# Two low parts of weight slabs made by GpSimd instead of VectorE in the latent attention

## The chip, the cores and the metric

The kernel runs on one core of a Trainium2 chip. The metric is the time of one execution in microseconds (us), the median of several runs. TensorE multiplies matrices, VectorE (DVE in the profile), ScalarE (ACT) and GpSimd (POOL) work on tiles in the on-chip memory SBUF, and SyncE (SP) issues transfers. VectorE and ScalarE also read PSUM, TensorE's eight result banks ps0 to ps7. The engines run side by side and wait for one another by semaphores only.

## The reference

It is a small transformer of two blocks over 256 tokens of width 1024, all in float32. The part that matters here is the first layer of the first block: eight heads of neighbourhood attention and eight heads of dense "latent" attention, joined and multiplied by an output weight. Beside it the second block's memory is normalized and projected.

```python
def dense_attention(q, k, v, scale):
    ...
        sc = jnp.einsum('bqhd,bkhd->bhqk', qi, k, preferred_element_type=jnp.float32) * scale
        p = jax.nn.softmax(sc, axis=-1)
        return jnp.einsum('bhqk,bkhd->bqhd', p.astype(v.dtype), v)
...
    return jnp.concatenate([out_a, out_b], axis=-1) @ w_o
...
        mkv = rms_norm_2(mem, mem_norm_gain[l]) @ w_mem_kv[l]
```

## The kernel before, in words

**Weights in slabs.** All weights pass through SBUF in 192 slabs of up to 128 x 2048 numbers, in the order of `weight_plan`. SyncE loads slab n into `raw[n % 5]`, once the products that used slab n - 5 are done. float32 products are made in two parts: ScalarE copies the slab to the reduced format as its high part (`whi`, L1230, three buffers), and the difference raw - whi is the low part (`wlo`, five buffers). VectorE makes it in one instruction of 128 x 2048 (L1720 in its `low`), or GpSimd in four of 128 x 512 (L2486 in its own `low`). `pooled(n)` says which of the two makes slab n's: in the kernel before GpSimd makes those of the last two slabs of `od_o`, most of `branch`, and all of `out2` and `fg`, all far behind the stage of the change. TensorE multiplies high by high, high by low and low by high (L595).

**When.** Each engine's program is written out by hand, and every step calls `ahead(n)`, which makes the parts of slab n + 2. A call for a slab that the engine doesn't make issues nothing. Slabs 10, 12, 15 and 17 (`EVO`) are the output weight of the first layer, and 11, 13, 14 and 16 (`MEM`) the memory's weight. So slab 14 is the third memory slab and slab 15 the third output slab.

**The attention around them.** Sixteen heads ("units" 0 to 15; from 8 on they are latent) pass in 19 steps s. Scores of a pair of units (L792 on TensorE); row maxima from PSUM (L1795 on VectorE for the latent ones); exponentials (L1296, ScalarE); one reciprocal and two multiplications of 128 x 256 per unit by 1/sum, from SBUF to SBUF (L1801, L1804 `TENSOR_SCALAR`, VectorE); transposes (L800, TensorE); a copy of the transposed probabilities from PSUM (VectorE's L1812 for odd units, ScalarE's L1305 for even ones); weighted values (L843, TensorE); outputs as a high part (L1326, ScalarE) and a low part (L1826, VectorE). Between these lie the products: step 11 multiplies slab 12 in four blocks, which VectorE adds to the residual (`onto`, L1868, reading PSUM), step 13 slab 13, step 15 slab 14, step 16 slab 15. The eight PSUM banks are handed out in turn, and TensorE takes one only when its last result has been read.

VectorE makes the low part of slab 14 in step 11, between the second and third block of slab 12, and that of slab 15 in step 13:

```python
                        if j == 2 and k < 3:
                            ahead(EVO[k])
                        onto(EVO[k], j, j)
```

Of the kernel before, what the change touches and what calls it, by code (L numbers as in the profile page):

```python
# [330 lines left out]
EVO = (10, 12, 15, 17)  # L331
MEM = (11, 13, 14, 16)
# [4 lines left out]
def build(nc, A, out):  # L337
    with ExitStack() as ctx:
# [124 lines left out]
        def pooled(n):  # L463

            name = plan[n][0]
            if name == "od_o":
                return n >= ODO + 2
            if name == "branch":
                return sum(p[0] == "branch" for p in plan[:n]) > 1
            return name in ("out2", "fg")  # L470
# [101 lines left out]
        def tensor(pe):  # L572
# [626 lines left out]
            for n in range(FF + 2, FD):  # L1199
                beside(n, x, late=pooled(n))  # L1200
                if n - FF in (4, 8, 12, 16):
                    rows_in((n - FF - 4) // 4)
# [509 lines left out]
        def vector(dve):  # L1712
            once = Once(dve)

            def low(n):
                if not split(n) or pooled(n):
                    return
                once.wait_ge(*at(("raw", n)))
                once.wait_ge(*at(("whi", n)))
                dve.tensor_tensor(wlo_of(n), raw_of(n), f32(whi_of(n)), ALU.subtract).then_inc(*tell(s_wlo, ("wlo", n)))  # L1720
# [754 lines left out]
        def gpsimd(pool):  # L2475
            once = Once(pool)

            def low(n):
                if not split(n) or not pooled(n):
                    return  # L2480
                once.wait_ge(*at(("raw", n)))
                once.wait_ge(*at(("whi", n)))
                lo, r, hi = wlo[n % RAW], raw[n % RAW], whi[split_at(n) % PARTS]
                for q in range(4):
                    v = slice(512 * q, 512 * q + 512)
                    m = pool.tensor_tensor(lo[:, v], r[:, v], f32(hi[:, v]), ALU.subtract)  # L2486
                m.then_inc(*tell(s_pool_wlo, ("wlo", n)))

            def ahead(n):
                for k in ahead_of(n):  # L2490
                    low(k)
# [49 lines left out]
                pool.tensor_tensor(QM[64:96, n, :], r[v, 0:256], r[v, 256:512], ALU.add).then_inc(*tell(s_pool, ("qr", n)))  # L2541
            once.wait_ge(*at(("qr", 7)))

            for n in (EVO[2], MEM[3], EVO[3]):
                ahead(n)
            for j in range(1, 4):
                add_square("n1", 0, j, j == 3)
# [44 lines left out]
            n = BLENDS  # L2592
# [90 lines left out]
        for program in (tensor, scalar, vector, gpsimd, sync):  # L2683
            program(silent)
# [8 lines left out]
        @block.gpsimd  # L2693
        def _(e):
            gpsimd(e)
# [39 lines left out]
```

## Time and profile before

| | |
|---|---|
| median of 3 runs | 1195.06 us (1194.7 to 1195.49) |
| the profiled execution | 1195.08 us |
| its span | 1193.3 us, TensorE clock granted 0.999 |
| TensorE busy | 1184.5 us |
| VectorE, ScalarE, GpSimd busy | 830.7, 658.5, 222.3 us |

The span runs from the first to the last instruction; 1.8 us of the execution lie around it. All times in rows are counted from the span's start. The latent attention with the memory's products beside it lies between about 80 and 150 us.

### The profile page before, as it was taken

How to read it: one execution, taken by the hardware profiler on the slowest of the kernel's cores; microseconds unless marked ns; L12 is line 12 of the kernel's file. 1: busy time of each engine (PE TensorE's matmuls, PEld its weight loads, DVE VectorE, ACT ScalarE, POOL GpSimd, SP SyncE). 2: the span in 40 equal slices, each digit the busy share in tenths (PEclk: the TensorE clock that was granted, in tenths of full speed). 3: DMA queues.
4: the chain of work that ended last, by engine and by line, in shares of the span. 5: the costliest groups of instructions: out<-in, count | busy, mean ns of one | idle time of the engine just before them, and what ended most of it. 6: DMA issues, size and time to landing. Idle time of an engine off the chain costs nothing.

```text
span 1193.3 us, 18415 instructions
## 1 busy us (share of the span) xinstructions
PE 1184.5 (99%) x7409; PEld 1034.6 (87%) x7409; DVE 830.7 (70%) x1184; ACT 658.5 (55%) x899; POOL 222.3 (19%) x169
## 2 busy tenths in 40 slices
PE   9999999999999999999999999999999999999998
PEld 9989898888898888888988888897878899888886
DVE  7878777754576688765788844597966566676863
ACT  5584465533455655557565535456685555555452
POOL 2530010000011021200300000010010885544100
PEclk9999999999999999999999999999999999999999
DMA  9723456656558566664366565555544455565551
GB/s 265 244 83 130 141 177 186 203 178 205 182 165 273 187 211 193 202 204 140 110 190 198 178 204 184 185 183 176 178 144 166 149 194 177 182 195 188 176 195 53
DMA packets 158995, 214.04 MB, mean 179 GB/s; under 512 B 5259, under 2 KB 111054, under 8 KB 158910
## 3 DMA queue, kind: packets, MB, share of 16 engines
q1 hardware_dynamic: 158110, 211.41, 54.6%
q8 instruction: 59, 0.97, 0.3%
q10 hardware_dynamic: 608, 0.99, 0.3%
q0 software_dynamic: 192, 0.46, 0.2%
q14 instruction: 26, 0.21, 0.1%
HBM read 205.50 MB, written 1.05 MB: 173 GB/s over the span
## 4 chain that ended last, share of the span: by engine, by line
PE 93%; DVE 4%; ACT 2%; issue 1%; DMA 1%; SPq 0%; DVEq 0%; ACTq 0%
PE ps L595 44%; PE ps L610 22%; PE ps L615 11%; PE ps L695 4%; PE ps L792 2%; PE ps L843 2%; PE ps L637 2%; PE ps L800 1%; DVE wlo L1720 1%; PE ps L811 1%; PE ps L661 1%; ACT whi L1230 1%; DMA raw<-in_ev_w_in_dram 1%; DVE TA L2400 0%; PE ps L716 0%
## 5 line engine op out<-in xcount | busy, mean ns | idle before, releaser
L1720 DVE TENSOR_TENSOR wlo<-raw,whi 128x2048 fp32r<-128x2048 f32 (+1 forms) x167 | 384.5, 2304 | 148.9 <-ACT whi L1230 148.3
L1230 ACT ACTIVATE whi<-raw 128x2048 fp32r<-128x2048 f32 x188 | 357.9, 1907 | 154.4 <-PE ps L595 132.3
L610 PE MATMUL ps<-XHL,whi 128*128 128x512 f32 x1248 | 311.1, 393 | 0.0
L610 PEld LDWEIGHTS ps<-XHL,whi 128*128 128x128 f32 x1248 | 225.3, 189 | 42.1 <-DVE BIG L2132 0.5
L615 PEld LDWEIGHTS ps<-XHL,wlo 128*128 128x128 f32 x1248 | 167.8, 190 | 11.8 <-DVE wlo L1720 1.1
L615 PE MATMUL ps<-XHL,wlo 128*128 128x256 f32 x1248 | 171.5, 282 | 0.3 <-DVE wlo L1720 0.2
L2486 POOL TENSOR_TENSOR wlo<-raw,whi 128x512 fp32r<-128x512 f32 x88 | 119.1, 1388 | 157.3 <-ACT whi L1230 157.1
L595 PE MATMUL ps<-whi,HL 128*128 128x512 f32 (+1 forms) x416 | 144.8, 373 | 0.0
L595 PE MATMUL ps<-whi,HH 128*128 128x512 f32 x384 | 143.3, 390 | 0.0
L595 PE MATMUL ps<-whi,XHL 128*128 128x512 f32 (+1 forms) x480 | 139.7, 378 | 0.0
L595 PE MATMUL ps<-wlo,HH 128*128 128x512 f32 x368 | 139.4, 389 | 0.0
L595 PEld LDWEIGHTS ps<-whi,XHL 128*128 128x128 f32 x480 | 85.9, 188 | 15.9 <-issue 0.7
L2562 POOL TENSOR_TENSOR TB<-TB,BIG 128x512 f32<-128x512 f32 x24 | 38.6, 1607 | 324.3 <-DVE BIG L2126 189.1
L595 PEld LDWEIGHTS ps<-whi,HL 128*128 128x128 f32 x416 | 76.1, 188 | 13.6
L595 PE MATMUL ps<-wlo,XHL 128*128 128x512 f32 (+1 forms) x240 | 87.8, 375 | 0.0
L595 PEld LDWEIGHTS ps<-whi,HH 128*128 128x128 f32 x384 | 71.9, 188 | 14.7
L595 PEld LDWEIGHTS ps<-wlo,HH 128*128 128x128 f32 x368 | 69.0, 188 | 14.6 <-DVE wlo L1720 0.4
L1286 ACT ACTIVATE TB<-ps 128x256 f32<-128x256 f32 x82 | 29.3, 378 | 58.0 <-PE ps L615 56.2
L1286 ACT ACTIVATE TA<-ps 128x256 f32<-128x256 f32 x66 | 23.4, 380 | 57.5 <-PE ps L615 45.1
L595 PEld LDWEIGHTS ps<-wlo,XHL 128*128 128x128 f32 x240 | 44.2, 188 | 8.3
L1861 DVE TENSOR_TENSOR TA<-ps,TB 128x256 f32<-128x256 f32 x56 | 23.2, 421 | 25.0 <-ACT TB L1286 24.7
L1296 ACT ACTIVATE SN<-SN,stat 128x384 f32<-128x384 f32 (+2 forms) x64 | 34.4, 544 | 10.1 <-DVE stat L1789 10.1
(281 smaller groups left out, 1652.6 us busy)
## 6 DMA issues: line engine op xcount, KB each, us to landing
raw<-in_mlp_w_dram SPq DMA_DIRECT2D x64, 1024.0 KB, 5.3
raw<-in_od_w_in_dram SPq DMA_DIRECT2D x36, 1024.0 KB, 5.4
raw<-in_w_in_dram SPq DMA_DIRECT2D x24, 1024.0 KB, 5.1
raw<-in_w_ffn_gate_dram SPq DMA_DIRECT2D x12, 1024.0 KB, 5.1
raw<-in_w_ffn_up_dram SPq DMA_DIRECT2D x12, 1024.0 KB, 5.1
raw<-in_w_ffn_down_dram SPq DMA_DIRECT2D x12, 1024.0 KB, 5.0
TB<-TA SPq DMA_DIRECT2D x96, 64.0 KB, 2.4
raw<-in_w_branch_dram SPq DMA_DIRECT2D x6, 1024.0 KB, 4.9
```

Source lines behind the costliest of these rows:

```text
L595: m = pe.matmul(to, l[c][a], r[c][b], start=first and k == 0, stop=last and k == 3 * n - 1)
L610: pe.matmul(b[m][:, :], w[m][c][0], XHL[:, c, :], start=c == 0, stop=False)
L615: i = pe.matmul(b[m][:, 0:S], w[m][c][1], x[c][0], start=False, stop=c == 7)
L637: i = pe.matmul(b[:, m * S:m * S + S], w[m][c][a], x[c][z], start=m == c == a == z == 0, stop=m == a == 1 and c == len(x) - 1)
L695: i = pe.matmul(b[n][:, m * S:m * S + S], h[a], x[c][z], start=m == c == a == z == 0, stop=m == 1 and c == 7 and z == 1)
L792: m = pe.matmul(banks[u][rows, lo:hi], l, r, start=start, stop=stop)
L1230: act.activation(whi_of(n), raw_of(n), ACT.Copy, scale=1.0).then_inc(*tell(s_whi, ("whi", n)))
L1286: act.activation(to[:, m * S:m * S + S], b[:, S:2 * S], ACT.Copy, scale=1.0).then_inc(*tell(s_act_out, ("copy", n, m)))
L1296: m = act.activation(to[:, lo:hi], src[:, lo:hi], ACT.Exp, bias=st[:, k:k + 1], scale=-1.0 if biased else 1.0, accum_out=st[:, 2 + k:3 + k])
L1720: dve.tensor_tensor(wlo_of(n), raw_of(n), f32(whi_of(n)), ALU.subtract).then_inc(*tell(s_wlo, ("wlo", n)))
L2486: m = pool.tensor_tensor(lo[:, v], r[:, v], f32(hi[:, v]), ALU.subtract)
L2562: pool.tensor_tensor(z, z, twice(RP[:, S:512]), ALU.mult).then_inc(*tell(s_pool, ("sine", k)))
```

## The change

`pooled` also names slabs 14 (`EVO[1] + 2`) and 15 (`MEM[1] + 2`). GpSimd's program calls `ahead(12)` and `ahead(13)` behind its last job in the latent attention, which issues these two low parts, four instructions each. The three calls that stood there, for slabs 17 to 19, issued nothing, as GpSimd made none of them. VectorE's calls stay and issue nothing for 14 and 15 now.

```diff
@@ -465,6 +465,8 @@
             name = plan[n][0]
             if name == "od_o":
                 return n >= ODO + 2
+            if n in (EVO[1] + 2, MEM[1] + 2):
+                return True
             if name == "branch":
                 return sum(p[0] == "branch" for p in plan[:n]) > 1
             return name in ("out2", "fg")
@@ -2541,7 +2543,7 @@
-            for n in (EVO[2], MEM[3], EVO[3]):
+            for n in (EVO[1], MEM[1]):
                 ahead(n)
             for j in range(1, 4):
                 add_square("n1", 0, j, j == 3)
```

All line numbers behind L466 grow by two. On VectorE, in step 11, this stands before: the scaling of unit 11, the four additions of slab 12's blocks with the low part of slab 14 (wlo4) between them, and the maxima of unit 12.

```order
L1804 TENSOR_SCALAR SN<-SN,stat 128x256 [waits s_dve]
L1804 TENSOR_SCALAR SN<-SN,stat 128x256
L1868 TENSOR_TENSOR XT<-XT,ps1 128x512 [waits s_product]
L1868 TENSOR_TENSOR XT<-XT,ps2 128x512 [waits s_product,s_dve_out]
L1720 TENSOR_TENSOR wlo4<-raw4,whi0 128x2048 [waits s_whi,s_raw4,s_dve_out]
L1868 TENSOR_TENSOR XT<-XT,ps3 128x512 [waits s_product]
L1868 TENSOR_TENSOR XT<-XT,ps4 128x512 [waits s_product,s_dve_out]
L1795 TENSOR_REDUCE stat<-ps5 128x1 [waits s_soft,s_score,s_dve_out]
```

And in the changed kernel, at the same place:

```order
L1806 TENSOR_SCALAR SN<-SN,stat 128x256 [waits s_dve]
L1806 TENSOR_SCALAR SN<-SN,stat 128x256
L1870 TENSOR_TENSOR XT<-XT,ps1 128x512 [waits s_product]
L1870 TENSOR_TENSOR XT<-XT,ps2 128x512 [waits s_product,s_dve_out]
L1870 TENSOR_TENSOR XT<-XT,ps3 128x512 [waits s_product,s_dve_out]
L1870 TENSOR_TENSOR XT<-XT,ps4 128x512 [waits s_product,s_dve_out]
L1797 TENSOR_REDUCE stat<-ps5 128x1 [waits s_soft,s_score,s_dve_out]
```

The low part is gone from VectorE and nothing else has moved; the same holds for slab 15 (wlo0) two steps on. On GpSimd the place between the queries' rotary sums (32x256) and the squares of the next norm (SQ) now has the two low parts:

```order
L2543 TENSOR_TENSOR BIG<-TB1 32x256 [waits s_pool] x3
L2488 TENSOR_TENSOR wlo4<-raw4,whi0 128x512 [waits s_whi,s_raw4,s_pool]
L2488 TENSOR_TENSOR wlo4<-raw4,whi0 128x512 x3
L2488 TENSOR_TENSOR wlo0<-raw0,whi1 128x512 [waits s_whi,s_raw0]
L2488 TENSOR_TENSOR wlo0<-raw0,whi1 128x512 x3
L2500 TENSOR_TENSOR SQ<-SQ 128x512 [waits s_square]
```

Before, the first and the last of these rows (L2541 and L2498 there) stood side by side. TensorE's order is the same in both kernels but for two semaphores. This is its stretch from the values of units 8 and 9 to the start of slab 13, in the kernel before:

```order
L843 MATMUL ps7<-PT,BIG 64x256 x3
L800 MATMUL ps0<-ident,SN 128x128 [waits s_soft]
L800 MATMUL ps0<-ident,SN 128x128 x3
L800 MATMUL ps1<-ident,SN 128x128 [waits s_soft,s_dve_out]
L800 MATMUL ps1<-ident,SN 128x128 x3
L595 MATMUL ps2<-HL,whi2 128x256 [waits s_whi,s_dve_out]
L595 MATMUL ps2<-HL,wlo3 128x256 [waits s_wlo]
```

The transposes of unit 11 (ps1) and slab 13's first product (ps2) wait for `s_dve_out`, which VectorE's additions above raise. Moved is only what TensorE waits for at the first low product of slabs 14 and 15: `s_pool_wlo` in place of `s_wlo`.

## Rows read from the trace of the kernel before

**Rows 1.** The page: busy time, share and instructions of each engine.

```profile
PE 1184.5 (99%) x7409; PEld 1034.6 (87%) x7409; DVE 830.7 (70%) x1184; ACT 658.5 (55%) x899; POOL 222.3 (19%) x169
```

**Rows 2.** Waits of TensorE, 84 to 160 us: total, times, longest.

```profile
PE ps L843 <- DVE PT L1812: 1.1, 2, 0.8
```

**Rows 3.** Timeline of TensorE: start, duration (us), instructions [idle before].

```profile
108.46 1.89 PE L792 MATMUL ps<-BIG 96*128 96x256 f32 x8
...
110.29 1.08 PE L843 MATMUL ps<-PT,BIG 128*64 128x256 f32 x8
111.30 1.09 PE L800 MATMUL ps<-ident,SN 128*128 128x128 f32 x8
112.15 0.36 PE L595 MATMUL ps<-HL,whi 128*128 128x256 f32 x1
...
117.99 1.89 PE L792 MATMUL ps<-BIG 96*128 96x256 f32 x8
120.18 1.08 PE L843 MATMUL ps<-PT,BIG 128*64 128x256 f32 x8 [0.30 <-DVE PT L1812]
121.20 1.09 PE L800 MATMUL ps<-ident,SN 128*128 128x128 f32 x8
...
128.88 1.08 PE L843 MATMUL ps<-PT,BIG 128*64 128x256 f32 x8 [0.85 <-DVE PT L1812]
```

**Rows 4.** Timeline of VectorE, 105 to 117 us.

```profile
105.55 2.29 DVE L1720 TENSOR_TENSOR wlo<-raw,whi 128x2048 fp32r<-128x2048 f32 x1
...
109.15 0.62 DVE L1804 TENSOR_SCALAR SN<-SN,stat 128x256 f32<-128x256 f32 x2
...
110.41 1.40 DVE L1868 TENSOR_TENSOR XT<-XT,ps 128x512 f32<-128x512 f32 x2
111.84 2.29 DVE L1720 TENSOR_TENSOR wlo<-raw,whi 128x2048 fp32r<-128x2048 f32 x1
114.06 1.40 DVE L1868 TENSOR_TENSOR XT<-XT,ps 128x512 f32<-128x512 f32 x2
115.49 1.42 DVE L1795 TENSOR_REDUCE stat<-ps 128x1 f32<-128x256 f32 x4
```

**Rows 5.** Timeline of VectorE, 120 to 129 us.

```profile
120.14 0.62 DVE L1804 TENSOR_SCALAR SN<-SN,stat 128x256 f32<-128x256 f32 x2
...
120.87 0.62 DVE L1804 TENSOR_SCALAR SN<-SN,stat 128x256 f32<-128x256 f32 x2
121.40 2.28 DVE L1720 TENSOR_TENSOR wlo<-raw,whi 128x2048 fp32r<-128x2048 f32 x1
...
124.20 1.41 DVE L1795 TENSOR_REDUCE stat<-ps 128x1 f32<-128x256 f32 x4
...
128.06 0.68 DVE L1812 COPY PT<-ps 128x512 f32<-128x512 f32 x1
```

**Rows 6.** Timeline of ScalarE: the high parts of slabs 13, 14 and of 15.

```profile
103.52 3.70 ACT L1230 ACTIVATE whi<-raw 128x2048 fp32r<-128x2048 f32 x2
...
118.84 1.94 ACT L1230 ACTIVATE whi<-raw 128x2048 fp32r<-128x2048 f32 x1
```

**Rows 7.** Timeline of GpSimd, 0 to 300 us: its next job.

```profile
152.45 1.30 POOL L2498 TENSOR_TENSOR SQ<-SQ 128x512 f32<-128x512 f32 x1 [72.29 <-ACT SQ L1246]
```

**Rows 8.** Timeline of GpSimd and VectorE side by side, 928 to 943 us.

```profile
928.42 10.07 POOL L2486 TENSOR_TENSOR wlo<-raw,whi 128x512 fp32r<-128x512 f32 x8 [49.33 <-ACT whi L1230]
...
928.23 1.64 DVE L1804 TENSOR_SCALAR SN<-SN,stat 128x256 f32<-128x256 f32 x2
930.84 0.42 DVE L1826 TENSOR_TENSOR OL<-ps,OH 128x256 fp32r<-128x256 f32 x1 [0.98 <-ACT OH L1326]
...
939.84 1.29 POOL L2486 TENSOR_TENSOR wlo<-raw,whi 128x512 fp32r<-128x512 f32 x1
...
940.24 1.44 DVE L2314 TENSOR_TENSOR BIG<-BIG,TB 128x512 f32<-128x512 f32 x1
...
941.10 1.75 POOL L2486 TENSOR_TENSOR wlo<-raw,whi 128x512 fp32r<-128x512 f32 x1
```

## The prediction

> **What bounds the kernel now.** I read the page's busy times first: TensorE is busy 1184.5 us of the 1193.3 us span, GpSimd 222.3 us [rows 1]. So nothing that shortens work on another engine pays unless TensorE waits for it. The change lies in the latent attention, so the next view is who TensorE waited for there, from 84 to 160 us: two waits, 1.1 us together, both of L843 (probabilities times values) for DVE's L1812, which copies transposed probabilities out of PSUM [rows 2]. The third view is TensorE in order of time [rows 3], where starts give each wait its size. Where it does not wait, the values follow the scores by 110.29 - 108.46 = 1.83 us; the next time by 120.18 - 117.99 = 2.19, so the first wait cost 0.36. A slab of this shape takes 117.99 - 112.15 = 5.84 us. The next slab starts 0.85 after the L800 of 121.20 (112.15 - 111.30), at 122.05, and ends at 127.89; the values start at 128.88, so the second wait cost 0.99. The sum, 1.35 us, is all that a faster DVE could win here; before and after these two TensorE goes on without a break.
>
> **What is removed.** Two DVE subtractions of 2.3 us, at 111.84 [rows 4] and at 121.40 [rows 5]. Both lie ahead of row maxima (L1795), on which the exponentials, the weighted values and then the late copy depend: 115.49 leads to the copy that L843 waits for at 120.18, and 124.20 to that of 128.06. Without anything else both copies would be some 2.2 us earlier and both waits gone.
>
> **What is added.** Eight GpSimd subtractions of a quarter slab. Their like appears later: eight in a row take 10.07 us, 1.26 each [rows 8], so a low part takes about 5.0 us in place of 2.29. They begin when ScalarE has written the high part: 103.52 + 3.70 = 107.22 for slab 14, and 118.84 + 1.94 = 120.78 for slab 15 [rows 6]. The low parts would be there by about 113 and 127; their slabs are multiplied from 122.05 and 130. So TensorE does not wait for GpSimd itself. The three removed calls of `ahead` issued no instruction, and GpSimd's next job starts at 152.45 after 72 us of idling [rows 7]: nothing is queued behind the new work. The change moves no DMA; weight loads are freed by the same products as before.
>
> **What it costs: DVE's scalings are held.** This is the term that I think decides. In [rows 8] a pair of L1804 (probabilities times 1/sum, SBUF to SBUF) takes 1.64 us beside a GpSimd subtraction, against 0.62 (109.15) without [rows 4]: the second of the pair ended at 928.23 + 1.64 = 929.87, 0.16 after the GpSimd instruction that was running (928.42, and 1.29 long as those at 939.84: 929.71). L2314, two SBUF inputs, ended at 941.68, 0.55 after the GpSimd instruction that began 0.4 us before it (939.84 + 1.29 = 941.13); the next GpSimd instruction ended at 942.85, 1.17 after L2314. L1826, which reads PSUM, took 0.42 in the middle of GpSimd's row. So DVE instructions with all operands in SBUF and GpSimd's subtractions take turns, one at a time, and those on PSUM pass. The Trainium skill says the same and more strictly (SBUF — State Buffer, "SBUF: two separate sides"): the pair of ports that the two engines share is an exclusive lock, held for the whole instruction, and the loser fully blocks. The trace agrees, with the 1.64 us above. Read at its worst, with each of four scalings held for a whole GpSimd instruction (4 x 1.26 = 5.0 us), the rule would give 2.2 us more than the sum below.
>
> First slab. DVE's previous subtraction ends at 105.55 + 2.29 = 107.84 [rows 4], after ScalarE's part, so GpSimd's first instruction really starts there and ends at 107.84 + 1.17 = 109.01. The first L1804 is issued at 109.15, when the second GpSimd instruction has begun (ends 110.27):
> - L1804 first: ends 110.27 + 0.15 = 110.42; GpSimd third: 110.42 + 1.17 = 111.59
> - L1804 second: 111.74; GpSimd fourth: 112.91
> - L1804 third: 113.06; the fourth finds GpSimd done and the next DVE instruction starts at 113.25.
> In the profile that next one (L1868, `onto`) starts at 110.41. So DVE is 2.84 us late there, and the 2.22 us saved behind it (114.06 - 111.84) leave it 0.62 late at the maxima: four L1868 of 0.715 bring 116.11 for 115.49.
>
> What waits for it: TensorE's order puts the transposes of unit 11 into bank ps1 and slab 13 into ps2, and takes each only after the first and the second L1868 have read it. The second ends at 113.25 + 0.71 + 0.68 = 114.64. Slab 13 started at 112.15 [rows 3], some 0.3 after its bank was freed by the L1868 that had ended by 111.84; TensorE follows a DVE result here after 0.14 (128.06 + 0.68 to 128.88). So slab 13 starts at 114.78: TensorE is 2.63 us late.
>
> What it gets back. The scores come at 117.99 + 2.63 = 120.62 and the values may start at 122.45; the copy L1812 had ended 0.14 before 120.18 and is only 0.62 late (120.66), so the first wait of 0.36 vanishes: 2.27 late. The second low part starts at about 120.9 + 0.62 on GpSimd, some 0.05 us after the third of four L1804 (120.87, [rows 5]), which shift by the same 0.62, as both hang on the same maxima. I take it that the fourth alone is held, by 1.02 as in [rows 8] (1.64 - 0.62). It then ends at 121.49 + 0.62 + 1.02 = 123.13, and the transposes that need it are due at 121.20 + 0.44 + 2.27 = 123.91: hidden by TensorE's own delay. The maxima come at 124.20 - 2.20 + 0.62 + 1.02 = 123.64 and the copy 3.86 (128.06 - 124.20) later, at 127.50, done by 128.2; slab 14 ends at 127.89 + 2.27 = 130.16. No wait: the second one (0.99) is gone too, and TensorE is 1.28 late. From there to the end it is busy without a break, with DVE and ScalarE ahead of it, so 1.28 us stays.
>
> Sum: +2.63 - 0.36 - 0.99 = +1.28. The profiled execution took 1195.08 us (span 1193.3 and 1.8 around it), the median of the runs is 1195.06, so I forecast **1196.3 us**. The bounds: nothing is held, -1.35; three or four scalings are held the second time too, +2.7 (below).
>
> **Rivals.**
> - *Banks free early enough.* If slab 13 waits only for the last scaling (113.33 + 0.14, then 0.43 of transposes: 113.90), TensorE is 1.75 late; 1.39 after the first wait is gone, and the transposes due at 121.20 + 0.44 + 1.39 = 123.03 wait 0.24 for 123.27. Less 0.99: +0.64, 1195.7 us. Against it: the order shows the wait of slab 13's first product for DVE's outputs.
> - *The engines don't disturb each other.* Both waits vanish, -1.35, 1193.7 us. For it: most DVE instructions here read PSUM, and 1.64 us in [rows 8] is one pair. Against it: the four scalings stand exactly where GpSimd starts.
> - *Held twice: slower.* The place is the second low part. If GpSimd's first instruction comes ahead of the softmax of unit 12 instead of just behind its third scaling, three are held, 2 x 1.02 more: the last ends at 125.17, and the transposes, due at 123.91, start at 125.31. TensorE is 2.27 + 1.40 = 3.67 late, and with the second wait gone 2.7: 1197.8 us. It decides if ScalarE is 0.8 us earlier against DVE (120.92 to 120.14); one scaling more, for which 0.06 us are enough, is +1.7 (1196.8). For it: 0.06 us is nothing. Against 0.8: the two move together.
> - *No effect at all*: held and hidden anyway, 1195.1 us. It would need slack at 112 us, where TensorE has none: the transposes started at 111.30, the scalings had ended 0.8 before.
>
> **How the numbers follow.** Forecast with its neighbours (1195.9 to 1196.9) 0.66; banks free early 0.10; undisturbed 0.10; held twice 0.08; no effect 0.06. The range of 8 in 10 takes in the first, the second and the last, and leaves out the undisturbed one and held twice: 1195.0 to 1197.3. What a measurement can tell here is about 0.2%, 2.39 us. The gain can't reach it, as TensorE's waits give 1.35 at most: faster 0.02 for what I overlook. Slower needs 2.39: held twice, 0.08. Same: 0.90.
>
> **What would show it.** L1804 near 109 as two pairs of about 2.4 and 1.5 us instead of 0.62; GpSimd's eight L2488 in two groups of about 5.1 us, near 108 and 121.5; TensorE's slab 13 starting about 2.6 us later, with a wait for DVE at L800 or the slab; no wait of L843 for L1812 at either place (L1814 now); everything from 130 us on shifted alike, by 1.3. I am wrong if L1804 keeps its 0.62, if TensorE waits for GpSimd's low parts at L597, or if the shift at 130 us differs from that at the end.

## The result

The changed kernel takes 1197.46 us (median of 20 runs, 1196.7 to 1199.46), the kernel before 1195.11 in the same series (20 runs, 1194.3 to 1196.56): a ratio of 1.002, 95% interval 1.0014 to 1.0027. It is 2.35 us slower where 1.28 was forecast, and just outside the range, which ended at 1197.3. The profiled execution took 1197.19 us (span 1195.4, 1.8 around it), 2.11 more than that of before.

**What became of TensorE and VectorE.** The page of the changed kernel, busy time of each engine:

```profile
PE 1185.3 (99%) x7409; PEld 1034.2 (87%) x7409; DVE 831.0 (70%) x1182; ACT 658.4 (55%) x899; POOL 232.8 (19%) x177
```

Against [rows 1] GpSimd has its eight instructions more, and VectorE two fewer. TensorE is 99% busy again, so the page alone tells nothing. The waits of TensorE from 84 to 160 us (total, times, longest), which answer to [rows 2]:

```profile
PE ps L802 <- DVE XT L1870: 1.5, 1, 1.5
PE ps L802 <- DVE SN L1806: 0.3, 1, 0.3
```

Both waits of L845 (L843 before) for the copy are gone, and two new ones stand at the transposes. TensorE in order of time (start, duration, instruction, idle before), against [rows 3]:

```profile
110.28 1.08 PE L845 MATMUL ps<-PT,BIG 128*64 128x256 f32 x8
111.68 0.66 PE L802 MATMUL ps<-ident,SN 128*128 128x128 f32 x4 [0.32 <-DVE SN L1806]
113.81 0.66 PE L802 MATMUL ps<-ident,SN 128*128 128x128 f32 x4 [1.47 <-DVE XT L1870]
114.53 0.39 PE L597 MATMUL ps<-HL,whi 128*128 128x256 f32 x1
...
120.38 1.89 PE L794 MATMUL ps<-BIG 96*128 96x256 f32 x8
122.20 1.08 PE L845 MATMUL ps<-PT,BIG 128*64 128x256 f32 x8
...
129.99 1.08 PE L845 MATMUL ps<-PT,BIG 128*64 128x256 f32 x8
```

Slab 13 starts at 114.53 for 112.15, 2.38 later. The values start at 122.20 for 120.18, 2.02 later: 0.36 came back. Those of 129.99 are 1.11 late. VectorE shows why (against [rows 4, 5]):

```profile
109.13 2.50 DVE L1806 TENSOR_SCALAR SN<-SN,stat 128x256 f32<-128x256 f32 x2
111.55 0.15 DVE L1803 RECIPROCAL stat<-stat 128x2 f32<-128x2 f32 x1
111.73 1.43 DVE L1806 TENSOR_SCALAR SN<-SN,stat 128x256 f32<-128x256 f32 x2
113.08 2.84 DVE L1870 TENSOR_TENSOR XT<-XT,ps 128x512 f32<-128x512 f32 x4
115.96 1.42 DVE L1797 TENSOR_REDUCE stat<-ps 128x1 f32<-128x256 f32 x4
...
120.60 0.62 DVE L1806 TENSOR_SCALAR SN<-SN,stat 128x256 f32<-128x256 f32 x2
121.13 0.16 DVE L1803 RECIPROCAL stat<-stat 128x2 f32<-128x2 f32 x1
121.33 1.63 DVE L1806 TENSOR_SCALAR SN<-SN,stat 128x256 f32<-128x256 f32 x2
```

and GpSimd's two new groups in the same execution:

```profile
107.38 5.37 POOL L2488 TENSOR_TENSOR wlo<-raw,whi 128x512 fp32r<-128x512 f32 x4 [27.21 <-ACT whi L1232]
121.38 5.21 POOL L2488 TENSOR_TENSOR wlo<-raw,whi 128x512 fp32r<-128x512 f32 x4 [8.64 <-ACT whi L1232]
```

The first four scalings take 2.50 and 1.43 us in place of 0.62 a pair, the second time one pair takes 1.63. One by one, the first three last 1.22, 1.35 and 1.17 us and end 0.15 us behind the end of a GpSimd instruction each (110.20, 111.48, 112.75); the fourth finds GpSimd done and takes 0.34. No semaphore stands between these instructions, so semaphores are not the only way in which engines hold each other up here. Up to 130 us the forecast's mechanism is what happened, with 1.11 us for 1.28. The text had said that everything behind would be shifted alike and that it was wrong if the shift at the end differed. It does: TensorE is 1.1 us late until 1099 us and 2.11 us late from 1106.

**Where the second microsecond goes.** Four views of the changed kernel near 1096 us: VectorE, GpSimd, ScalarE, TensorE.

```profile
1092.99 2.29 DVE L1722 TENSOR_TENSOR wlo<-raw,whi 128x2048 fp32r<-128x2048 f32 x1
1095.20 0.69 DVE L2419 TENSOR_TENSOR HL<-TB,HH 128x512 fp32r<-128x512 f32 x1
1096.27 0.76 DVE L1863 TENSOR_TENSOR TB<-ps,TB 128x256 f32<-128x256 f32 x2 [0.38 <-ACT TB L1288]
1097.06 1.77 DVE L2410 TENSOR_TENSOR TB<-TA,TB 128x512 f32<-128x512 f32 x1
...
1095.69 5.56 POOL L2488 TENSOR_TENSOR wlo<-raw,whi 128x512 fp32r<-128x512 f32 x4 [5.86 <-ACT whi L1232]
...
1095.46 0.64 ACT L1288 ACTIVATE TB<-ps 128x256 f32<-128x256 f32 x2
1098.87 0.63 ACT L1658 ACTIVATE HH<-TB 128x512 fp32r<-128x512 f32 x1 [2.78 <-DVE TB L2410]
...
1108.50 0.74 PE L617 MATMUL ps<-XHL,wlo 128*128 128x256 f32 x4 [0.80 <-DVE wlo L1722]
```

The same place in the kernel before:

```profile
1094.33 0.68 DVE L2417 TENSOR_TENSOR HL<-TB,HH 128x512 fp32r<-128x512 f32 x1
1095.05 0.76 DVE L1861 TENSOR_TENSOR TB<-ps,TB 128x256 f32<-128x256 f32 x2
1095.84 0.88 DVE L2408 TENSOR_TENSOR TB<-TA,TB 128x512 f32<-128x512 f32 x1
...
1094.83 5.55 POOL L2486 TENSOR_TENSOR wlo<-raw,whi 128x512 fp32r<-128x512 f32 x4 [5.88 <-ACT whi L1230]
...
1096.76 0.64 ACT L1656 ACTIVATE HH<-TB 128x512 fp32r<-128x512 f32 x1 [1.53 <-DVE TB L2408]
...
1106.39 1.21 PE L615 MATMUL ps<-XHL,wlo 128*128 128x256 f32 x8 [0.24 <-DVE wlo L1720]
```

In the changed kernel VectorE has a pause of 0.38 us ahead of L1863. The profile puts it down to ScalarE's L1288, but that had ended at 1096.10 and its first half earlier: the record of VectorE's wait for it ends at 1095.87, and L1863 starts 0.40 us behind that record, where the kernel before has 0.045 at the same place. Without the pause L2410 (both inputs in SBUF) meets the end of GpSimd's first quarter and takes 0.88; 0.38 later it meets the second quarter and is held as the scalings are: 1.77. ScalarE's HH, behind it, comes at 1098.87 for 1096.76, 1.25 us more than GpSimd's own shift there (0.86). ScalarE's and then VectorE's part of the next slab follow. TensorE, 1.13 us late against the kernel before until 1099 us, is 1.54 late at 1102, as its products there (L612) stretch by 0.41 behind the later ScalarE; then it waits 0.80 us for a low part instead of 0.24 and is 2.11 late. That is the whole 1.0.

What I then saw in counting: the instruction after the pause is the 1600th record of VectorE in the trace (its waits on semaphores are records too, so two low parts fewer are three records fewer, 1708 for 1711); the 1088th, 512 earlier, starts 0.4 us late too (hidden). Before, the 1600th is a low part three records earlier in the program, and starts on time, while the instruction ahead of it is still running. A third place shows the same in both kernels: the 448th record starts 0.41 us behind its wait's record before (300.46 us) and 0.40 in the changed kernel (303.39), though it is a different instruction of the program. The view of the DMA queues shows a packet on the queue for instruction code near either place (us 1098 to 1099 in the changed kernel; its columns are packets, MB, share of 16 engines):

```profile
q14 instruction: 1, 0.01, 2.1%
```

and from 1092 to 1093 us in the kernel before:

```profile
q14 instruction: 1, 0.01, 2.3%
```

The packet of the changed kernel lies between 1098.6 and 1099 us, more than 2 us behind the end of the pause (1096.27), and only14 below has one at 1094.3 without any pause near it. So the packets don't show that VectorE paused for code.

That made the theory for the late part: VectorE can pause at fixed numbers of its stream, and removing two instructions moves such a number onto a place where a pause costs. That it pauses for new code is a guess.

A third thing hides in the spread of the times. Of the 20 runs of the changed kernel seven have a mean granted clock of 0.998 or less and a median of 1198.46; the other thirteen have 1197.19. Of the kernel before, five of 66 runs in the two series below were so low, and not slower for it; a low mean is a sign of a clock drop, no proof. The profile of the changed kernel has no such drop; two of the kernels below were caught with one.

### The profile page after: what moved, and what is told of

It is laid out like the page before. It is cut to its first block, busy times and chain, and to the rows that moved or that the text cites. A ratio compares the mean times of both kernels' runs of the same rounds, so it can differ in the third digit from the quotient of the medians.

```text
span 1195.4 us, 18421 instructions
## 1 busy us (share of the span) xinstructions
PE 1185.3 (99%) x7409; PEld 1034.2 (87%) x7409; DVE 831.0 (70%) x1182; ACT 658.4 (55%) x899; POOL 232.8 (19%) x177
## 4 chain that ended last, share of the span: by engine, by line
PE 92%; DVE 3%; ACT 1%; DMA 1%; SPq 1%; issue 1%; DVEq 0%; ACTq 0%
PE ps L597 44%; PE ps L612 22%; PE ps L617 11%; PE ps L697 4%; PE ps L794 2%; PE ps L845 2%; PE ps L639 2%; PE ps L802 1%; DMA raw<-in_ev_w_in_dram 1%; ACT whi L1232 1%; PE ps L813 1%; DVE wlo L1722 1%; DVE TA L2402 0%; SPq L2640 0%; PE ps L1105 0%
## 5 line engine op out<-in xcount | busy, mean ns | idle before, releaser
L1722 DVE TENSOR_TENSOR wlo<-raw,whi 128x2048 fp32r<-128x2048 f32 (+1 forms) x165 | 379.9, 2304 | 148.2 <-ACT whi L1232 147.5
L612 PE MATMUL ps<-XHL,whi 128*128 128x512 f32 x1248 | 311.4, 393 | 0.2
L612 PEld LDWEIGHTS ps<-XHL,whi 128*128 128x128 f32 x1248 | 225.3, 189 | 42.5 <-ACT BIG L1672 0.5
L2488 POOL TENSOR_TENSOR wlo<-raw,whi 128x512 fp32r<-128x512 f32 x96 | 129.7, 1383 | 194.1 <-ACT whi L1232 193.9
L1288 ACT ACTIVATE TB<-ps 128x256 f32<-128x256 f32 x82 | 29.2, 377 | 58.0 <-PE ps L617 56.2
L1288 ACT ACTIVATE TA<-ps 128x256 f32<-128x256 f32 x66 | 23.4, 380 | 57.3 <-PE ps L617 45.0
L1863 DVE TENSOR_TENSOR TA<-ps,TB 128x256 f32<-128x256 f32 x56 | 23.2, 421 | 25.0 <-ACT TB L1288 24.7
```

The lines of the kernel that those rows point to most:

```text
L612: pe.matmul(b[m][:, :], w[m][c][0], XHL[:, c, :], start=c == 0, stop=False)
L1288: act.activation(to[:, m * S:m * S + S], b[:, S:2 * S], ACT.Copy, scale=1.0).then_inc(*tell(s_act_out, ("copy", n, m)))
```

## The experiments

Each kernel has 11 runs beside 33 of the kernel before on the same chip: 1195.00 us for the first four kernels, 1195.03 for the last four.

**only14: the first slab alone.** Against the changed kernel:

```diff
-            if n in (EVO[1] + 2, MEM[1] + 2):
+            if n == EVO[1] + 2:
```

> Only slab 14's low part goes to GpSimd; slab 15's stays on DVE. The collision theory: the four scalings near 109 us are held as in the changed kernel (pairs of about 2.5 and 1.4 us instead of 0.62), slab 13 starts 2.4 us late, both of TensorE's waits for the copies go, and TensorE is 1.0 to 1.1 us late at 130 us, like the changed kernel. If the engines did not disturb each other, it would be 0.36 us early there instead. Whether the end is as late as 130 us is the second question: if delays only add up, the time is 1196.2; if the later stages add the 1.2 us by which the changed kernel's median exceeds its shift at 130 us, it is 1197.4.

Measured: 1196.64 us (1195.76 to 1197.81), ratio 1.0012 (1.0003 to 1.0021). The waits near 112 us are the same 1.5 and 0.3 us. One instruction fewer instead of two puts the 1600th record on L2419, without a pause, and no wait of 0.8 us comes late (its 1088th record, a low part, does start 0.4 us late, hidden). But the profiled execution shows something else, in the table by stretch (busy time of each engine, then granted clock, DMA share, GB/s):

```profile
112.00:114.00 2.00, 0.65 (x4) 0.42 (x4) 1.97 (x4) 0.00 (x0) 0.28 (x1) 1.00 0.20 82
114.00:119.00 5.00, 4.94 (x29) 4.93 (x29) 2.80 (x7) 2.72 (x11) 0.00 (x0) 0.66 0.00 0
```

TensorE was busy 0.65 of 2.00 us, in its wait for L1870; then the granted clock averages 0.66 over five microseconds: half speed (the 1.2 GHz level) for 3.41 us from 114.61, with slab 13 under way. This execution loses 1.5 us more by it (TensorE, against the kernel before, from the start of slab 13 to the next scores). Five of the 11 runs have the low mean clock (median 1197.01), the others have 1196.06, which is +1.06, the theory's number. The split by clock was made after the runs were seen; the median of all 11 lies between the two forecasts.

**only15: the second slab alone.**

```diff
-            if n in (EVO[1] + 2, MEM[1] + 2):
+            if n == MEM[1] + 2:
```

> Only slab 15's low part goes to GpSimd; slab 14's stays on DVE. The collision theory: the scaling pair at 120.87 us takes 1.64 instead of 0.62, so the transposes of unit 13 start 1.0 us late, and the wait of 0.99 us for the copy near 128 us goes: no shift at 130 us, 1195.1 us. Without a disturbance the second wait alone would go: -0.99, 1194.1 us.

Measured: 1195.04 us (1194.02 to 1196.84), ratio 1.0 (0.9992 to 1.0009). TensorE's waits from 84 to 160 us:

```profile
PE ps L802 <- DVE SN L1806: 0.8, 1, 0.8
PE ps L845 <- DVE PT L1814: 0.3, 1, 0.3
```

One pair of scalings takes 1.62 us, the transposes wait 0.8 for it, and the late wait of L845 is paid for by that. So the second slab alone is worth nothing; in the changed kernel its cost is hidden by the lateness that the first one makes.

**after_scaling: GpSimd begins behind the scalings.** What disturbs is taken away, by order and not by size:

```diff
-            for n in (EVO[1], MEM[1]):
+            for n, u in ((EVO[1], 11), (MEM[1], 13)):
+                once.wait_ge(*at(("soft", u)))
                 ahead(n)
```

> Both low parts on GpSimd as in the changed kernel, but GpSimd starts each only when the scaling of units 10 and 11, and of 12 and 13, is done. The collision theory: L1806 keeps 0.62 us, the first low part runs from about 110.6 to 115.7, the second from 119.4 to 124.5, nothing of DVE's in these stretches has all its operands in SBUF, both waits of TensorE (1.35 us) go: 1193.7 us. If what costs is something else that a GpSimd subtraction does to DVE or to TensorE wherever it stands, it stays near the changed kernel's 1197.5.

Measured: 1194.99 us (1194.36 to 1196.91), ratio 0.9999 (0.999 to 1.0008). GpSimd's two groups in its timeline:

```profile
111.16 5.03 POOL L2488 TENSOR_TENSOR wlo<-raw,whi 128x512 fp32r<-128x512 f32 x4 [30.44 <-DVE SN L1806]
119.88 5.00 POOL L2488 TENSOR_TENSOR wlo<-raw,whi 128x512 fp32r<-128x512 f32 x4 [3.69 <-DVE SN L1806]
```

Every pair of scalings has its 0.62 again, GpSimd its 5.0, and TensorE waits for nothing from 84 to 160 us. Yet the median is that of before. In its profile TensorE gains 1.28 us on the kernel before between 108 and 129 us, and loses 1.21 between 1099 and 1107: this kernel has the same two instructions fewer on VectorE, its 1600th record is L1863 too, and it has the late wait:

```profile
1106.84 1.22 PE L617 MATMUL ps<-XHL,wlo 128*128 128x256 f32 x8 [0.79 <-DVE wlo L1722]
```

**late_te_1: a late TensorE and nothing else.** On the kernel before, ten transposes more, to see whether lateness alone grows on its way to the end:

```diff
-                for to, of in turns_of(u):
+                for to, of in (turns_of(u) * 4)[2:] if u == 15 else turns_of(u):
```

> The kernel before, with the transposes of unit 15 (near 136 us) done 3.5 times over: ten more of 0.11 us, which delay TensorE by 1.1 us there and touch nothing else; nothing moves to GpSimd. If delays only add up, 1196.2 us. If it is TensorE's lateness against the other engines that makes the later stages lose more, as the profile of the changed kernel shows near 1100 us, about 1197.4 us.

Measured: 1196.04 us (1195.72 to 1198.11), ratio 1.0009 (1.0 to 1.0018). The 1.1 us stays 1.04 us. A delay near 136 us is neither absorbed nor enlarged, so the late microsecond of the changed kernel does not follow from a late TensorE alone.

**before_three_fewer: the kernel before with three fewer instructions on VectorE.** Neither slab is moved; three softmaxes are scaled by one instruction of 512 columns in place of two of 256, which gives their second half the first half's factor.

```diff
-                for j, (lo, hi) in enumerate(parts_of(u)):
+                for j, (lo, hi) in enumerate(((0, 2 * S),) if u in (7, 8, 9) else parts_of(u)):
```

> The kernel before, without the change, in which the softmax scalings of units 7, 8 and 9 are one VectorE instruction of 128x512 each in place of two of 128x256 (the second half is then scaled by the first half's factor: the values differ, the work is the same). VectorE's instructions after 91 us have numbers lower by three, as in the changed kernel. Theory A: the 1600th recorded instruction is L1861 near 1094 us, it starts 0.38 us late, the second L2408 there takes 1.77 us, TensorE waits 0.8 us for wlo at L617, and the time is 1196.0 us, 1.0 above before. Theory B (the loss needs the two pooled slabs): 1195.0 us, and no such pause. The three shorter softmaxes themselves gain nothing that lasts, at most 0.2 us.

Measured: 1196.01 us (1195.27 to 1196.89), ratio 1.0007 (0.9998 to 1.0016); by the medians +0.98, and the interval, from 0.9998, takes in no difference at all, so the profile has to carry it. VectorE's timeline, and under it TensorE's waits after 1080 us:

```profile
1094.93 0.68 DVE L2417 TENSOR_TENSOR HL<-TB,HH 128x512 fp32r<-128x512 f32 x1
1096.03 0.76 DVE L1861 TENSOR_TENSOR TB<-ps,TB 128x256 f32<-128x256 f32 x2 [0.41 <-ACT TB L1286]
1096.82 1.76 DVE L2408 TENSOR_TENSOR TB<-TA,TB 128x512 f32<-128x512 f32 x1
```

```profile
PE ps L615 <- DVE wlo L1720: 0.8, 1, 0.8
PE ps L610 <- ACT BIG L1670: 0.4, 1, 0.4
```

Pause, held instruction and late waits are those of the changed kernel, in a kernel without the change. In this profile TensorE loses 1.24 us there (1099 to 1107 us), and the shorter scalings win 0.41 near 120 us, where the first wait for a copy is gone: more than the 0.2 allowed for. So the forecast of +1.0 was met in part by luck: two errors of about 0.2 us offset each other.

**after_pad: the changed kernel with the numbers put back.** Three memsets of one column, which the trace shows at 117.72 us, 0.08 us together, in a stretch of 2.1 us where VectorE waits for ScalarE anyway (ahead of the L1828 of group 4, L1832 in this kernel):

```diff
+                if gs[0] == 4:
+                    for i in range(3):
+                        dve.memset(spare[:, i:i + 1], 0.0)
                 once.wait_ge(*at(("ohi", gs[-1])))
```

> The changed kernel with three tiny VectorE instructions (memsets of 128x1 in a tile nobody reads, without a wait) put ahead of an L1828 early in the run, so that VectorE's later instructions have the numbers that they had before the change. Theory A (VectorE pauses for some 0.38 us ahead of its 1600th recorded instruction; in the changed kernel that is L1863 near 1096 us, and TensorE loses about 1.0 us by it; with the pad the 1600th is a scaling or a low part that ends hidden, as before): L1863 starts without the pause, the second L2410 near 1096 us takes 0.88 us and not 1.77, TensorE doesn't wait for wlo at L617, and the time is 1196.3 us, about 1.0 below the changed kernel's 1197.2 (in executions without a drop of the clock). Theory B (the late loss belongs to the lateness of 1.1 us itself or to the changed order of GpSimd and VectorE there): the pause and the wait of 0.8 stay, 1197.3 us.

Measured: 1196.95 us (1195.93 to 1198.12), ratio 1.0016 (1.0007 to 1.0024). That median lies between the two forecasts, and the runs split by their clock: five runs at a clock of 0.999 lie between 1195.93 and 1196.19 (median 1196.03, +1.0), six at 0.998 or less have 1197.86. Late, TensorE waits for nothing:

```profile
1097.04 0.69 DVE L2423 TENSOR_TENSOR HL<-TB,HH 128x512 fp32r<-128x512 f32 x1
1097.77 0.76 DVE L1867 TENSOR_TENSOR TB<-ps,TB 128x256 f32<-128x256 f32 x2
1098.56 0.88 DVE L2414 TENSOR_TENSOR TB<-TA,TB 128x512 f32<-128x512 f32 x1
```

So the pad gives back 1.16 us in the executions without a clock drop (1197.19 to 1196.03, over two series whose kernels before differ by 0.08). The profiled execution is one with the drop, 3.41 us at half clock from 115.25, and TensorE loses 1.5 us by it:

```profile
112.00:114.00 2.00, 0.66 (x4) 0.42 (x4) 1.96 (x5) 0.00 (x0) 1.15 (x1) 1.00 0.67 272
114.00:119.00 5.00, 4.72 (x25) 4.49 (x26) 3.66 (x11) 1.85 (x9) 0.00 (x0) 0.66 0.00 0
```

**after_pad_filled: the long wait filled.** On top of after_pad, TensorE repeats the transposes of unit 10 into their own bank:

```diff
-                for to, of in turns_of(u):
+                for to, of in (turns_of(u) * 5)[2:] if u == 10 else turns_of(u):
```

> after_pad, and TensorE repeats the four transposes of unit 10 until 18 stand there (14 more, at 0.107 us each 1.5 us) in place of most of its wait of 1.5 us near 112 us. VectorE copies them only near 120 us, so nothing is held by them. Theory A (the half clock that some executions of the changed kernel and of only14 show for 3.4 us from 114.6 us follows TensorE's long wait): at most one of the 11 runs has a mean clock below 0.9985, where about four of 11 had it with the wait, and the median is that of the executions without a drop, 1196.2 us; after_pad's median lies up to 1 us above its lower runs. Theory B (the clock falls by chance or because of the work of VectorE and GpSimd): as many low clocks as in after_pad. If the fill ends later than the wait did, the time is above after_pad's by that much, at most 0.2 us.

Measured: 1196.10 us (1194.9 to 1197.08), ratio 1.001 (1.0001 to 1.0019). One run of 11 has a clock of 0.998, and it is not a slow one (1195.76). The stretches that read 0.66 above:

```profile
112.00:114.00 2.00, 1.66 (x16) 1.21 (x13) 1.97 (x3) 0.00 (x0) 1.98 (x2) 1.00 0.99 408
114.00:119.00 5.00, 4.93 (x42) 4.51 (x40) 4.49 (x13) 1.02 (x5) 0.00 (x0) 1.00 0.03 10
```

With fourteen transposes that compute nothing new the median is 0.85 us lower than after_pad's; the two intervals overlap, and it is no lower than after_pad's runs without a drop (1196.03), as it should be if the fill only prevents the drop. With the long wait 18 of 42 runs have the low clock (changed kernel 7 of 20, only14 5 of 11, after_pad 6 of 11); filled 1 of 11; in the five other kernels of this study, none with that wait, 6 of 55. Against the 55 the excess is plain; against the single series of 11 it is likely and not more.

**after_scaling_pad: both repairs.** after_scaling with the same three memsets.

> The kernel in which GpSimd's two slabs wait for the scalings of units 11 and 13 (after_scaling), with the same three tiny VectorE instructions. Theory A: the local gain of 1.3 us at 129 us is kept to the end, 1193.7 us against 1195.0 before and 1195.0 for after_scaling without the pad; no wait of L617 for wlo, and L2410 takes 0.88. Theory B: it stays at 1195.0.

Measured: 1194.06 us (1193.32 to 1194.66), ratio 0.999 (0.9981 to 0.9999), no run with a low clock. VectorE's L2414 has its 0.88 again and TensorE's only wait after 1080 us is that of the kernel before:

```profile
PE ps L618 <- DVE wlo L1723: 0.2, 1, 0.2
```

It is 0.97 us faster than before and 3.4 faster than the changed kernel, with the same two low parts on GpSimd: less than the 1.3 expected, more than nothing, and the fastest kernel of the study. In its profile TensorE wins 1.27 us between 108 and 129 us and loses nothing behind; where the other 0.3 of the median went is not shown.

## Why the prediction was right about the place and wrong about the size

The mechanism at 109 to 130 us was right step by step.

- **The scalings are held.** Forecast as pairs of about 2.4 and 1.5 us, measured 2.50 and 1.43; the next instruction 2.84 us late, measured 113.08 for 110.41, 2.67. The Trainium skill (SBUF — State Buffer, "SBUF: two separate sides") calls the shared pair of ports an exclusive lock for a whole instruction. The trace agrees, and adds that the two engines then take turns one for one: four scalings, three of them held, cost 3.93 - 1.24 = 2.69 us more, not 4 x 1.26. That the order is the cause and not GpSimd's presence is shown by after_scaling: same instructions, 0.62 a pair.
- **Slab 13.** Forecast 2.63 late, measured 2.38: VectorE's addition ended 0.16 earlier than forecast (114.48), and TensorE followed it after 0.05 and not 0.14. The wait stands at the transposes of unit 11 (1.47 for L1870, after 0.32 for the scalings). The rival in which the banks come free early (1.75) is out.
- **Second slab.** One scaling held for 1.01, hidden, and no wait of L845: as forecast in the changed kernel. only15 shows what it costs without that cover: 0.8.
- **What comes back.** Both waits, as forecast; 1.11 net for 1.28.

The step that failed is the last: "From there to the end it is busy without a break, with DVE and ScalarE ahead of it, so 1.28 us stays." The first delay does stay (late_te_1), but two costs that come with the change, and that the sum put at nothing, arise outside it:

- **+1.0 us near 1096 us**, in both profiled kernels with those two VectorE instructions fewer and nothing in their place: a pause of 0.4 us that goes by the position in VectorE's stream, and an instruction that thereby meets GpSimd's next one. The kernel before with three instructions fewer has it, the changed kernel with three more has not. TensorE there is not "busy without a break", and VectorE and ScalarE are not ahead of it: it had a wait of 0.24 for that low part in the kernel before, and I had not looked.
- **+1.0 to +1.8 us in about four executions of ten**: slab 13 at half clock after the wait of 1.5 us. The forecast named the wait and priced it at its length only. In the median of 20 runs it makes 0.27 (1197.46 for 1197.19), if the runs with a low mean clock are the ones with a drop.

1.11 + 1.0 + 0.27 = 2.38, for 2.35 measured. What is shown is that the pause goes by the number and costs 1.0; what VectorE does in it stays open. That it loads code is a guess: the packets on the instruction queue come more than 2 us behind the pause. The Trainium skill (Runtime: NRT & Kernel Launch, "Instruction fetch mechanics") says that an engine's code is refilled in blocks of 256 instructions and that crossing a block is mostly hidden. The trace neither confirms nor refutes it: the pauses stand at the 448th, 1088th and 1600th record, 640 and 512 apart, which are multiples of 128 and not all of 256. All three stand right behind the record of a wait; at the same numbers in other kernels no gap shows where the record is itself a wait or comes right behind another instruction. The pause was 0.4 us on its engine, and 1.0 in this kernel. Why the clock falls in some executions and not in others stays open as well.

## What to carry to other kernels

When work moves from VectorE to GpSimd, ask which VectorE instructions with all operands in SBUF will stand beside it, and start GpSimd's job behind them with a semaphore: a wait that let GpSimd end its first low part 3.4 us later (116.19 for 112.75) turned a loss of 1.11 us at 129 us into a gain of 1.28. A change of one microsecond in a kernel of a thousand must be followed to the end of the trace, because the count of instructions alone can move a pause onto a critical place; a few idle instructions ahead tell whether it did. And where TensorE gets a new wait such as the 1.5 us here, look at the granted clock behind it and at the spread of the runs, not at one profile; filling the wait with repeated work may be cheaper than waiting.

## What the runs showed of the hardware

- VectorE starts about 0.4 us late at the 1088th and the 1600th of its records in the changed kernel, after_scaling and before_three_fewer, at the 1088th in only14, and at the 448th in the kernel before as well; in the kernel before and with the three memsets the 1088th record is a wait and the 1600th follows a running instruction, and no gap shows.
- VectorE's instructions with all operands in SBUF and GpSimd's subtractions alternate one for one: a pair of 128x256 scalings 2.50 us beside GpSimd, 0.62 without; a 128x512 addition 0.88 or 1.77, by 0.4 us of difference in its start.
- After a wait of TensorE of 1.5 us in a stretch that is otherwise full, the granted clock was at half for 3.41 us in both executions where it was caught (only14, after_pad), though not in the changed kernel's own profile, and the mean clock was low in 18 of 42 runs; with transposes in place of the wait in 1 of 11.
